# Second layer's heads: score and value products as three fp32r products, woven into the next head's value projection

## The chip, the cores and the metric

The kernel runs on one core of a Trainium2 chip. The metric is the device time of one execution in microseconds (us); of several executions the median counts.

## The reference, cut to what matters

The program runs four layers and then a second block over 256 latent and 256 context tokens of width 2048, all in f32. The change is in layer 1, a bidirectional mLSTM with 8 heads. Scores are 128 wide per head, values 256:

```python
def _mlstm_branch(h_lat, h_ctx, w_in, b_gate, hn, w_out, ctx_out):
    q, k, v, o, g, z = jnp.split(h @ w_in, idx, axis=-1)
    ...
    s = jnp.einsum('bhtd,bhsd->bhts', q, k) * jnp.exp(dmat - m_t[..., None])
    num = a[..., None] * jnp.einsum('bhtd,bhde->bhte', q, C) + jnp.einsum('bhts,bhse->bhte', s, v)
    den = a * jnp.einsum('bhtd,bhd->bht', q, n) + jnp.sum(s, axis=-1)
    h = num / jnp.maximum(jnp.abs(den), jnp.exp(-m_t))[..., None]
    ...
    y = jax.nn.sigmoid(o) * h
    y = _rmsnorm(y, hn)
    return (y * jax.nn.silu(z)) @ w_out
```

The scan over chunks is computed here as one masked product over all 512 tokens in each of the two directions (d = 0 forward, d = 1 backward): P = exp(cb + column) x (k q), masked, then P times [v, 1], whose last column is the denominator.

## The kernel before

Each engine has its own program, written out by hand; they meet in semaphores. `L.up(..., name)` marks an event, `w.wait_ge(L.at(name))` waits for it. An engine works strictly in the order in which its program is written.

**Projections.** Weights come in pieces of 1024 columns (half a 128x2048 block). A piece is loaded into WR, ScalarE rounds it to fp32r in WH (L1574), VectorE writes the rest WR - WH to WL (L2389); TensorE then makes three fp32r products of it with the activations HH and HL (`three`, L502 to L506, and `tproject`, L635 to L637). WH and WL hold three pieces (`NP` = 3), so a piece can be split only when TensorE is through with the third before it. `cut_to(n)` on ScalarE and VectorE splits all pieces below n; `along(job)` is `cut_to` of the job's last piece plus 3. One piece is 24 products of 512 columns.

**One head h on TensorE**, in order: two products that spread `cb` over a bank each (PS4, PS5; L1038), the score product S(h,0), z projection 2h, S(h,1), z projection 2h+1, S(h,2), q(h+1), S(h,3), k(h+1), then the value products (L1061: 20 of them, two directions for each of four token blocks tb, in banks PS4 to PS7 in turn), then `vo(h+1)` (values and output gate of the next head, 8 pieces, four banks at once), then eight transposes of the result M_HH (L1072). z, z, q, k take one accumulating bank each of PS0 to PS3, and `vo` takes all four: its fourth bank is that of k. `tproject` asks for all its banks, and waits for them, before its first product. Head 7 has no q, k and vo behind it.

**VectorE in a head**: `cb` plus a column into M_P (L2363), M_P times S out of PSUM (L2360, `mult` below), the splits, the drain of the value products (three small instructions for the denominator and one of 256 columns, L2366 or L2369, for each tb and direction), M_HH times the gate (L2360, 1024 columns), the norm (L2366), then the evacuation of the transposes (L2369) and of the values (L2372). Between them it works at `bg(n)`: n steps of the vector-matrix products for the modulations of later layers (L2411; two passes of 1024 columns a step while both the latent and the context vector need it, one pass in the last part). Each step's block of `ada_w` is loaded by SyncE into one of two buffers when the step before the last is through. ScalarE does the exps, tanhs, squares and the evacuation of q, k and the gate; GpSimd masks the diagonal blocks.

The four score blocks are called k = 0 to 3 (key block), with columns 0 to 512 for k < 2, 256 to 512 else.

## Time and profile before

| what | value |
|---|---|
| median of 3 runs | 2987.71 us (2981.6 to 2988.95) |
| the profiled execution's own time | 2990.57 us |
| its span, first to last instruction | 2988.8 us |
| TensorE busy | 2932.5 us (98%) |
| VectorE busy | 2090.1 us (70%) |
| ScalarE busy | 1178.0 us (39%) |
| granted TensorE clock | 0.996 of full speed |

Busy times are those of one execution; the value "idle before" counts gaps above 0.15 us. A matmul's duration is its latency; neighbours overlap, so what one costs is the distance of two starts.

### The profile page before, as it was taken

What the parts mean: (1) busy time and instruction counts of PE and PEld (TensorE: products, weight loads), DVE (VectorE), ACT (ScalarE), POOL (GpSimd) and SP (SyncE); (2) the same over time, 40 slices, a digit from 0 to 9 for tenths busy, and PEclk for the clock granted to TensorE, in tenths of its full rate; (3) what the DMA queues carried; (4) which work ended last, traced back from release to release, by engine and by line L of the source; (5) the groups of instructions that cost most, each with busy time, mean ns of one, the idle gap of its engine ahead of it and who ended that gap; (6) DMA issues with size and microseconds to landing.
All of it is one profiled execution on the core that took longest, in us unless ns stands there. A gap on an engine that the chain in (4) does not pass through costs nothing.

```text
span 2988.8 us, 43582 instructions
## 1 busy us (share of the span) xinstructions
PE 2932.5 (98%) x17098; PEld 2353.5 (79%) x17098; DVE 2090.1 (70%) x3957; ACT 1178.0 (39%) x2056; POOL 103.5 (3%) x188
## 2 busy tenths in 40 slices
PE   8999999999999999999999999999999999999999
PEld 7777778888888888878888888888888888885346
DVE  4576876788888776677666886677675678765455
ACT  4322323322332232242245555455444445543344
POOL 0000000000000000000000000000010120000000
PEclk9999999999999999999999999999999999999999
DMA  9777784354555455538636774645576443487997
GB/s 366 281 266 286 273 282 149 127 169 148 190 168 177 162 183 169 179 128 275 235 117 206 258 241 142 197 148 180 195 236 218 141 164 128 152 274 259 403 404 314
DMA packets 193197, 641.69 MB, mean 215 GB/s; under 512 B 21488, under 2 KB 36192, under 8 KB 192992
## 3 DMA queue, kind: packets, MB, share of 16 engines
q1 hardware_dynamic: 132080, 423.44, 40.6%
q10 hardware_dynamic: 58032, 207.12, 20.3%
q0 software_dynamic: 2880, 8.35, 0.9%
q8 instruction: 135, 2.21, 0.3%
q14 instruction: 70, 0.57, 0.1%
HBM read 624.15 MB, written 12.58 MB: 213 GB/s over the span
## 4 chain that ended last, share of the span: by engine, by line
PE 87%; DVE 7%; ACT 3%; DMA 2%; issue 1%; SPq 0%; DVEq 0%; ACTq 0%; POOL 0%; POOLq 0%
PE PS L506 15%; PE PS L502 11%; PE PS L504 9%; PE PS L505 9%; PE PS L635 7%; PE PS L637 7%; PE PS L636 7%; PE PS L1061 2%; PE PS L798 2%; PE PS L1472 2%; DMA AR<-e_w 1%; DVE WL L2389 1%; PE PS L1441 1%; PE PS L1428 1%; PE PS L1122 1%
## 5 line engine op out<-in xcount | busy, mean ns | idle before, releaser
L2389 DVE TENSOR_TENSOR WL<-WR,WH 128x1024 fp32r<-128x1024 f32 (+1 forms) x566 | 682.4, 1211 | 401.7 <-ACT WH L1574 400.5
L506 PE MATMUL PS<-HT,WL 128*128 128x256 f32 (+1 forms) x2928 | 951.5, 325 | 0.0
L1574 ACT ACTIVATE WH<-WR 128x1024 fp32r<-128x1024 f32 (+1 forms) x566 | 587.1, 1044 | 873.1 <-PE PS L506 486.7
L506 PEld LDWEIGHTS PS<-HT,WL 128*128 128x128 f32 x2928 | 552.1, 189 | 47.6
L502 PE MATMUL PS<-HT,WH 128*128 128x512 f32 x1584 | 566.0, 401 | 9.2 <-DVE WL L2389 6.1
L504 PE MATMUL PS<-HT,WH 128*128 128x512 f32 (+1 forms) x1344 | 518.4, 386 | 5.4 <-DVE HT L2369 2.4
L505 PE MATMUL PS<-HT,WH 128*128 128x512 f32 (+1 forms) x1344 | 507.9, 378 | 0.0
L635 PE MATMUL PS<-WH,HT 128*128 128x512 f32 x1016 | 402.7, 396 | 3.5 <-DVE HT L2369 2.5
L637 PE MATMUL PS<-WH,HT 128*128 128x512 f32 x1016 | 396.8, 391 | 0.0
L636 PE MATMUL PS<-WL,HT 128*128 128x512 f32 x1016 | 396.2, 390 | 0.0
L502 PEld LDWEIGHTS PS<-HT,WH 128*128 128x128 f32 x1584 | 297.4, 188 | 90.2 <-issue 13.1
L504 PEld LDWEIGHTS PS<-HT,WH 128*128 128x128 f32 x1344 | 253.1, 188 | 70.1 <-issue 14.6
L505 PEld LDWEIGHTS PS<-HT,WH 128*128 128x128 f32 x1344 | 253.3, 188 | 47.2 <-issue 1.7
L635 PEld LDWEIGHTS PS<-WH,HT 128*128 128x128 f32 x1016 | 191.3, 188 | 42.8 <-DVE HT L2369 2.1
L637 PEld LDWEIGHTS PS<-WH,HT 128*128 128x128 f32 x1016 | 191.1, 188 | 40.5
L636 PEld LDWEIGHTS PS<-WL,HT 128*128 128x128 f32 x1016 | 191.2, 188 | 38.2
L2411 DVE CUSTOM_DVE_ANT_0 WR<-WR,SCB,MOD 128x1024 f32<-128x1024 f32 x132 | 169.3, 1283 | 20.3 <-DMA WR<-ada_w 16.5
L2411 DVE CUSTOM_DVE_ANT_0 WR<-WR,SCB 128x1024 f32<-128x1024 f32 x132 | 161.4, 1223 | 23.5 <-DMA WR<-ada_w 19.9
L2369 DVE SCALAR_TENSOR_TENSOR YT<-PS,MOD,YT 128x256 f32<-128x256 f32 x126 | 57.9, 481 | 56.0 <-PE PS L506 54.5
L2411 DVE CUSTOM_DVE_ANT_0 JUNK<-WR,SCB,MOD 128x1024 bf16<-128x1024 f32 x68 | 87.0, 1280 | 4.0 <-DMA WR<-ada_w 1.9
L2411 DVE CUSTOM_DVE_ANT_0 JUNK<-WR,SCB 128x1024 bf16<-128x1024 f32 x68 | 83.0, 1220 | 5.9 <-DMA WR<-ada_w 3.4
L2360 DVE TENSOR_TENSOR AR<-AR 128x512 f32<-128x512 f32 (+9 forms) x140 | 74.3, 535 | 10.0 <-ACT AR L1705 1.2
(472 smaller groups left out, 3319.1 us busy)
## 6 DMA issues: line engine op xcount, KB each, us to landing
WR<-ada_w SPq DMA_DIRECT2D x264, 512.0 KB, 4.6
AR<-e_w SPq DMA_DIRECT2D x88, 512.0 KB, 10.0
E_RING<-e_w SPq DMA_DIRECT2D x80, 512.0 KB, 10.2
WR<-m_vo ACTq DMA_DIRECT2D x64, 512.0 KB, 4.6
WR<-a_qz ACTq DMA_DIRECT2D x64, 512.0 KB, 4.8
WR<-n_m SPq DMA_DIRECT2D x64, 512.0 KB, 4.3
AR<-ada_p ACTq DMA_DIRECT2D x56, 512.0 KB, 6.3
AR<-ada_p SPq DMA_DIRECT2D x48, 512.0 KB, 8.0
```

The source lines that it names most:

```text
L502: e.matmul(ps[:, 0:512], wh, HT[:, :, c, a:b], start=c == 0, stop=False)
L504: e.matmul(ps[:, 0:b - a], wh, HH_[:, c, a:b], start=c == 0, stop=False)
L505: e.matmul(ps[:, 0:b - a], wh, HL_[:, c, a:b], start=False, stop=False)
L506: return e.matmul(ps[:, 0:b - a], wl, HH_[:, c, a:b], start=False, stop=c == last)
L635: e.matmul(ps[:], HH_[:, c, t], wh[:, k, :], start=c == 0, stop=False)
L636: e.matmul(ps[:], HH_[:, c, t], wl[:, k, :], start=False, stop=False)
L637: i = e.matmul(ps[:], HL_[:, c, t], wh[:, k, :], start=False, stop=c == 15)
L798: i = e.matmul(ps[32 * k:32 * k + 32, 256 * half:256 * half + 256], S2Q[:, at:at + 32], wa[:, k, :], start=m == 0, stop=m == GP - 1)
L1574: e.activation(part_of(WH, s), place_of(plan["slot"][p])[:, 0:width(s)], ACT.Copy, scale=1.0).then_inc(*L.up(hi_done, ("hi", s)))
L2360: e.tensor_tensor(o, a, b, op).then_inc(*done(*names))
L2389: e.tensor_tensor(part_of(WL, s), place_of(plan["slot"][plan["split"][s]])[:, 0:width(s)], part_of(WH, s).bitcast(F32), ALU.subtract).then ...
L2411: e.tensor_tensor_reduce(out=o, in0=x, in1=SCB[:, v, k], scale=1.0, scalar=m if half else 0.0, op0=ALU.mult, op1=ALU.add, accum_out=m).the ...
```

## The change

The score product S(h,k) and each value product, plain f32 matmuls before, become three fp32r products of high and low parts (high x high, high x low, low x high). For that ScalarE writes high parts (M_QH, M_VH, M_PH) and VectorE low parts (M_QL, M_VL, M_PL: `q_low`, `k_low`, `lows`). The value products get 258 columns instead of 257. The four token blocks of value products are issued behind pieces 0 to 3 of `vo(h+1)`, no longer ahead of it. The addition of the column to `cb` goes from VectorE to ScalarE (Identity, or at once as bias of the exp), the masks are applied before the exp, the first direction's scaling (`first_way`) and the norm (`normed`) go to ScalarE; P is held only in the blocks that the mask leaves (M_BLOCKS, 2560 of 3072 columns). q and k have one buffer instead of two.

```diff
-    M_QK = [cv(1024, "p (a n) -> p a n", a=2) for _ in range(2)]
-    M_V = cv(4 * 257, "p (t n) -> p t n", t=4)
+    M_QH, M_QL = (ARR[:, 1024 * i:1024 * i + 1024].rearrange("p (a n) -> p a n", a=2) for i in range(2))
+    cv(2048)
+    cv(4 * 258)
     M_O = cv(1024, "p (t n) -> p t n", t=4)
     M_HH = cv(1024, "p (t n) -> p t n", t=4)
     M_P = [cv(1536) for _ in range(2)]
     M_E2 = cv(512)
+    M_VH, M_VL = (ARR[:, at:at + 1032].rearrange("p (t n) -> p t n", t=4) for at in (2048, 11784))
+    M_PH = [ARR[:, 8712 + 1536 * d:10248 + 1536 * d] for d in range(2)]
+    M_PL = [ARR[:, 5128 + 1536 * d:6664 + 1536 * d] for d in range(2)]
...
-            def vo(h):
-                tproject(("vo", h), I["m_vo"][h], 1, ALL, acc if h else wrk)
+            def vo(h, between=()):
+                tproject(("vo", h), I["m_vo"][h], 1, ALL, acc if h else wrk, between)
...
-                    w.wait_ge(L.at(("qe", h), ("ke", h)))
-                    e.matmul(ps[:, 0:512 - c0], qk[:, 1, 128 * k:128 * k + 128], qk[:, 0, c0:512], start=True,
-                             stop=True).then_inc(*L.up(mm_done, ("full", ("S", h, k)), ("qk_used", h)))
+                    w.wait_ge(L.at(("ql", h), ("kl", h)))
+                    o, t = ps[:, 0:512 - c0], slice(128 * k, 128 * k + 128)
+                    e.matmul(o, M_QH[:, 1, t], M_QH[:, 0, c0:512], start=True, stop=False)
+                    e.matmul(o, M_QH[:, 1, t], M_QL[:, 0, c0:512], start=False, stop=False)
+                    e.matmul(o, M_QL[:, 1, t], M_QH[:, 0, c0:512], start=False, stop=True).then_inc(
+                        *L.up(mm_done, ("full", ("S", h, k)), ("qk_used", h)))
...
-                for tb in range(4):
+                def value_products(tb):
                     for d in range(2):
                         ps = bank(4 + (2 * tb + d) % 4, ("pv", h, tb, d))
                         ks = M_KEYS[tb][d]
                         for m, k in enumerate(ks):
                             c = M_PC[k] + 128 * tb - (0 if k < 2 else 256)
-                            w.wait_ge(L.at(("p", h, k, d), ("ve", h), ("one", "v")))
-                            i = e.matmul(ps[:, 0:257], M_P[d][:, c:c + 128], M_V[:, k, :], start=m == 0,
-                                         stop=m == len(ks) - 1)
+                            ph, pl = M_PH[d][:, c:c + 128], M_PL[d][:, c:c + 128]
+                            w.wait_ge(L.at(("p", h, k, d), ("ve", h)))
+                            e.matmul(ps[:, 0:258], ph, M_VH[:, k, :], start=m == 0, stop=False)
+                            e.matmul(ps[:, 0:258], ph, M_VL[:, k, :], start=False, stop=False)
+                            i = e.matmul(ps[:, 0:258], pl, M_VH[:, k, :], start=False, stop=m == len(ks) - 1)
                         i.then_inc(*L.up(mm_done, ("full", ("pv", h, tb, d)), ("p_used", h), ("v_used", h)))
+
                 if h < 7:
-                    vo(h + 1)
+                    vo(h + 1, {tb: lambda tb=tb: value_products(tb) for tb in range(4)})
                 else:
+                    for tb in range(4):
+                        value_products(tb)
...
+                e.activation(M_QH[:, 0, :], place[("q", h)][:], ACT.Copy, scale=ASC).then_inc(*L.up(act_done, ("qe", h)))
...
+                e.activation(M_QH[:, 1, :], place[("k", h)][:], ACT.Copy, scale=1.0).then_inc(*L.up(act_done, ("ke", h)))
...
+                    e.activation(M_VH[:, tb, 0:256], place[("vo", h, tb)][:, 0:256], ACT.Copy, scale=1.0).then_inc(
+                        *L.up(act_done, ("vh", h, tb)))
                     e.activation(M_O[:, tb, :], place[("vo", h, tb)][:, 256:512], ACT.Tanh, scale=0.5).then_inc(
                         *L.up(act_done, ("oe", h), ("oe", h, tb), ("free", ("vo", h, tb))))
...
+                for d in range(2):
+                    ps, free = place[("cb", h, d)], ("free", ("cb", h, d))
+                    w.wait_ge(L.at(("full", ("cb", h, d))))
+                    for k in range(4):
+                        t = slice(128 * k, 128 * k + 128)
+                        e.activation(M_P[d][:, m_at(k, t.start, t.stop)], ps[:, t], ACT.Identity,
+                                     bias=M_ACOL[:, k, 32 * d + h:32 * d + h + 1], scale=1.0).then_inc(
+                            *L.up(act_done, ("pt", h, k, d), free))
+                    for k in range(4):
+                        for a, b in M_REST[k, d]:
+                            e.activation(M_P[d][:, m_at(k, a, b)], ps[:, a:b], ACT.Exp,
+                                         bias=M_ACOL[:, k, 32 * d + h:32 * d + h + 1], scale=1.0).then_inc(
+                                *L.up(act_done, ("pe", h, k, d), free))
                 for k in range(4):
-                    n = 512 if k < 2 else 256
                     for d in range(2):
-                        p = M_P[d][:, M_PC[k]:M_PC[k] + n]
-                        w.wait_ge(L.at(("pt", h, k, d)))
...
+                    for d in range(2):
+                        w.wait_ge(L.at(("pp", h, k, d)))
+                        for a, b in M_BLOCKS[k, d]:
+                            at = m_at(k, a, b)
+                            e.activation(M_PH[d][:, at], M_P[d][:, at], ACT.Copy, scale=1.0).then_inc(
+                                *L.up(act_done, ("ph", h, k, d)))
...
+                def first_way(tb):
+                    if h and tb == 0:
+                        w.wait_ge(L.at(("hh_used", h - 1)))
+                    w.wait_ge(L.at(("pvs", h, tb, 0)))
+                    e.activation(M_HH[:, tb, :], place[("pv", h, tb, 0)][:, 0:256], ACT.Copy,
+                                 scale=M_ST[2 * tb % 4][:, 0:1]).then_inc(
+                        *L.up(act_done, ("pvx", h, tb), ("free", ("pv", h, tb, 0))))
...
+                def normed():
+                    w.wait_ge(L.at(("yi", h)))
+                    for tb in range(4):
+                        e.activation(M_HH[:, tb, :], M_HH[:, tb, :], ACT.Copy, scale=s[:, 8 + tb:9 + tb]).then_inc(
+                            *L.up(act_done, ("yn", h, tb)))
...
+                    for q in range(8):
+                        cut_to(plan[("vo", h + 1)][0] + q + NP)
+                        if q < 4:
+                            first_way(q)
+                        elif q == 4:
+                            squares()
+                        elif q == 5:
+                            normed()
...
-                    copy(M_V[:, tb, 0:256], place[("vo", h, tb)][:, 0:256], ("ve", h), ("free", ("vo", h, tb)))
+                    w.wait_ge(L.at(("vh", h, tb), ("oe", h, tb)))
+                    tt(M_VL[:, tb, 0:256], place[("vo", h, tb)][:, 0:256], M_VH[:, tb, 0:256].bitcast(F32), ALU.subtract,
+                       ("ve", h), ("free", ("vo", h, tb)))
...
+            def q_low(h):
+                w.wait_ge(L.at(("qe", h)))
+                stt(M_QL[:, 0, :], place[("q", h)][:], ASC, M_QH[:, 0, :].bitcast(F32), ALU.mult, ALU.subtract, ("ql", h),
+                    ("free", ("q", h)))
+
+            def k_low(h):
+                w.wait_ge(L.at(("ke", h)))
+                tt(M_QL[:, 1, :], place[("k", h)][:], M_QH[:, 1, :].bitcast(F32), ALU.subtract, ("kl", h),
+                   ("free", ("k", h)))
...
+                def lows(k):
+                    for d in range(2):
+                        w.wait_ge(L.at(("ph", h, k, d)))
+                        for a, b in M_BLOCKS[k, d]:
+                            at = m_at(k, a, b)
+                            tt(M_PL[d][:, at], M_P[d][:, at], M_PH[d][:, at].bitcast(F32), ALU.subtract, ("p", h, k, d))
...
-                        p = M_P[d][:, M_PC[k]:M_PC[k] + 512 - c0]
-                        ts(p, place[("cb", h, d)][:, c0:512], M_ACOL[:, k, 32 * d + h:32 * d + h + 1], 0.0,
-                           ALU.add, ALU.min, ("pt", h, k, d), *([("free", ("cb", h, d))] if k == 3 else []))
...
+                        q_low(h + 1)
+                lows(3)
+                if h < 7:
+                    k_low(h + 1)
...
+                def drained(tb):
                     for d in range(2):
...
+                        recip(s, s, ("pvs", h, tb, d))
+                        if d:
+                            w.wait_ge(L.last(dve_done), L.at(("pvx", h, tb)))
                             stt(M_HH[:, tb, :], ps[:, 0:256], s, M_HH[:, tb, :], ALU.mult, ALU.add,
                                 ("free", ("pv", h, tb, d)))
...
+                    for q in range(8):
+                        cut_to(plan[("vo", h + 1)][0] + q + NP)
+                        if q < 4:
+                            drained(q)
+                        if q == 3:
+                            opened()
+                            bg(1)
+                        elif q == 5:
+                            inverse()
+                        bg(1)
...
-                        w.wait_ge(L.at(("pe", h, k, d)))
-                        e.affine_select(out=pd, in_=pd, compare_op=ALU.is_ge, fill=0.0, base=0,
+                        w.wait_ge(L.at(("pt", h, k, d)))
+                        e.affine_select(out=pd, in_=pd, compare_op=ALU.is_ge, fill=-3e38, base=0,
...
```

VectorE's program between k(h+1) and the drain, head 1. WL is a split, ISA a pass of `bg`, PS1 the bank of k(2), PS0 that of q(2). Before:

```order
L2389 TENSOR_TENSOR WL<-WR,WH 128x1024 [waits hi_done] x2
L2411 ISA JUNK,MOD<-WR,SCB,MOD 128x1024 [waits ada_done,adaw1_landed]
L2411 ISA MOD 128x1
L2411 ISA WR,MOD<-WR,SCB,MOD 128x1024 [waits ada_done]
L2411 ISA MOD 128x1
L2411 ISA JUNK,MOD<-WR,SCB 128x1024 [waits ada_done,adaw0_landed]
L2411 ISA MOD 128x1
L2411 ISA WR,MOD<-WR,SCB 128x1024 [waits ada_done]
L2411 ISA MOD 128x1
L2369 SCALAR_TENSOR_TENSOR SML<-PS4,SML 128x1 [waits mm_done]
```

and in the changed program:

```order
L2462 TENSOR_TENSOR WL<-WR,WH 128x1024 [waits hi_done] x2
L2484 ISA JUNK,MOD<-WR,SCB,MOD 128x1024 [waits ada_done,adaw1_landed]
L2484 ISA MOD 128x1
L2484 ISA WR,MOD<-WR,SCB,MOD 128x1024 [waits ada_done]
L2484 ISA MOD 128x1
L2484 ISA JUNK,MOD<-WR,SCB 128x1024 [waits ada_done,adaw0_landed]
L2484 ISA MOD 128x1
L2484 ISA WR,MOD<-WR,SCB 128x1024 [waits ada_done]
L2484 ISA MOD 128x1
L2442 SCALAR_TENSOR_TENSOR ARR<-PS0,ARR 128x512 [waits act_done]
L2433 TENSOR_TENSOR ARR<-AR,ARR 128x128 [waits act_done]
L2433 TENSOR_TENSOR ARR<-AR,ARR 128x256 [waits act_done]
```

Behind the last row stand the low part of k, which releases PS1, then a split, then the first drain. q's and k's low parts and the last low parts of P have moved in behind the two `bg` steps.

TensorE, from the last products of k(2) on. Before, the value products (L1061) followed, and vo (L635) behind them:

```order
L506 MATMUL PS1<-HT,WL 128x512
L1061 MATMUL PS4<-AR 128x257
L1061 MATMUL PS5<-AR 128x257 x2
L1061 MATMUL PS6<-AR 128x257 [waits dve_done]
L1061 MATMUL PS6<-AR 128x257
```

and in the changed program vo (L648) follows at once, with a wait for VectorE:

```order
L519 MATMUL PS1<-HT,WL 128x512
L648 MATMUL PS2<-WH,HT 128x512 [waits dve_done,lo_done]
L649 MATMUL PS2<-WL,HT 128x512
L650 MATMUL PS2<-WH,HT 128x512
L648 MATMUL PS2<-WH,HT 128x512
```

The value products now come 24 products later, and nothing stands between k and the wait for its bank.

ScalarE, the evacuation of vo, before:

```order
L1888 ACT_TABLE_LOAD
L1888 ACTIVATE AR<-PS2 128x256 [waits mm_done]
L1888 ACTIVATE AR<-PS3 128x256
L1888 ACTIVATE AR<-PS0 128x256
L1888 ACTIVATE AR<-PS1 128x256
```

and in the changed program, where the load of tanh's table has moved from ahead of the wait for vo to behind the first copy:

```order
L1909 ACTIVATE ARR<-PS2 128x256 [waits mm_done]
L1911 ACT_TABLE_LOAD
L1911 ACTIVATE AR<-PS2 128x256
L1909 ACTIVATE ARR<-PS3 128x256
L1911 ACTIVATE AR<-PS3 128x256
```

## Rows read from the trace of the kernel before

**Rows 1.** The page: busy time of two engines, and the chain that ended last

```profile
PE 2932.5 (98%) x17098; PEld 2353.5 (79%) x17098; DVE 2090.1 (70%) x3957; ACT 1178.0 (39%) x2056; POOL 103.5 (3%) x188
...
PE 87%; DVE 7%; ACT 3%; DMA 2%; issue 1%; SPq 0%; DVEq 0%; ACTq 0%; POOL 0%; POOLq 0%
```

**Rows 2.** Windows, two heads, two value stretches, a head's start, head 7

```profile
core 0: us, PE busy (x) PEld busy (x) DVE busy (x) ACT busy (x) POOL busy (x), PEclk, DMA share, GB/s
684.25:785.32 101.07, 100.49 (x444) 82.12 (x443) 82.72 (x148) 28.47 (x43) 3.41 (x9) 1.00 0.52 172
1188.81:1289.07 100.26, 100.26 (x444) 82.21 (x443) 61.68 (x113) 28.46 (x43) 3.41 (x9) 1.00 0.53 173
833.30:842.65 9.35, 8.77 (x42) 7.33 (x40) 8.31 (x32) 0.60 (x1) 0.00 (x0) 1.00 0.35 112
1236.80:1245.30 8.50, 8.50 (x42) 7.41 (x40) 6.21 (x28) 0.60 (x1) 0.00 (x0) 1.00 0.30 101
785.32:787.79 2.47, 2.47 (x13) 1.39 (x12) 1.84 (x4) 1.21 (x4) 0.98 (x1) 1.00 0.61 182
1302.55:1314.35 11.80, 10.49 (x48) 8.47 (x46) 9.84 (x37) 0.60 (x1) 0.00 (x0) 1.00 0.26 89
```

**Rows 3.** Timeline of TensorE, end of k(3), value products, start of vo(3)

```profile
start us, us, engine line op out<-in xcount [idle before <-releaser]
832.85 0.39 PE L505 MATMUL PS<-HT,WH 128*128 128x512 f32 x1
833.07 0.39 PE L506 MATMUL PS<-HT,WL 128*128 128x512 f32 x1
833.30 2.77 PE L1061 MATMUL PS<-AR 128*128 128x257 f32 x12
836.64 6.35 PE L1061 MATMUL PS<-AR 128*128 128x257 f32 x28 [0.58 <-DVE SML L2369]
842.65 0.58 PE L635 MATMUL PS<-WH,HT 128*128 128x512 f32 x1
```

**Rows 4.** Timeline of TensorE, fp32r products of 256 columns in another layer

```profile
1496.96 0.28 PE L710 MATMUL PS<-HT,WH 128*128 128x256 f32 x1
1497.08 0.28 PE L711 MATMUL PS<-HT,WH 128*128 128x256 f32 x1
1497.20 0.28 PE L712 MATMUL PS<-HT,WL 128*128 128x256 f32 x1
```

**Rows 5.** Timeline of ScalarE, evacuation of k(3)

```profile
833.50 0.60 ACT L1879 ACTIVATE AR<-PS 128x512 f32<-128x512 f32 x1 [4.32 <-PE PS L506]
```

**Rows 6.** Timeline of VectorE around k(3)'s end, a heavy head

```profile
829.21 1.23 DVE L2389 TENSOR_TENSOR WL<-WR,WH 128x1024 fp32r<-128x1024 f32 x1 [3.16 <-ACT WH L1574]
830.35 1.22 DVE L2411 CUSTOM_DVE_ANT_0 JUNK<-WR,SCB 128x1024 bf16<-128x1024 f32 x1
...
834.32 1.28 DVE L2411 CUSTOM_DVE_ANT_0 WR<-WR,SCB,MOD 128x1024 f32<-128x1024 f32 x1
835.52 0.08 DVE L2411 DVE_READ_ACCUMULATOR2_ANT MOD<- 128x1 f32 x1
835.52 0.15 DVE L2369 SCALAR_TENSOR_TENSOR SML<-PS,SML 128x1 f32<-128x1 f32 x1
...
836.50 0.15 DVE L2369 SCALAR_TENSOR_TENSOR SML<-PS,SML 128x1 f32<-128x1 f32 x1
```

**Rows 7.** Timeline of VectorE, instructions like the new ones

```profile
801.77 0.68 DVE L2369 SCALAR_TENSOR_TENSOR YT<-AR,PS 128x512 f32<-128x512 f32 x1
802.37 1.28 DVE L2360 TENSOR_TENSOR AR<-AR,PS 128x512 f32<-128x512 f32 x2
...
824.17 0.74 DVE L2360 TENSOR_TENSOR AR<-AR,PS 128x256 f32<-128x256 f32 x2
824.83 1.22 DVE L2389 TENSOR_TENSOR WL<-WR,WH 128x1024 fp32r<-128x1024 f32 x1
```

**Rows 8.** Timeline of VectorE around k(6)'s end (1136.55), a light head

```profile
1136.18 0.08 DVE L2411 DVE_READ_ACCUMULATOR2_ANT MOD<- 128x1 f32 x1
1137.18 0.16 DVE L2369 SCALAR_TENSOR_TENSOR SML<-PS,SML 128x1 f32<-128x1 f32 x1 [0.92 <-PE PS L1061]
```

**Rows 9.** The loads of ada_w from 600 to 1300 us

```profile
DMA to landing us min/median/max: 3.5/4.3/7.3
```

**Rows 10.** Timeline of VectorE behind the end of vo(2) at 785.32

```profile
785.95 1.41 DVE L2369 SCALAR_TENSOR_TENSOR YT<-PS,SML,YT 128x512 f32<-128x512 f32 x2 [0.97 <-PE PS L1072]
```

**Rows 11.** Timeline of ScalarE ahead of vo(1)'s evacuation

```profile
679.06 1.06 ACT L1574 ACTIVATE WH<-WR 128x1024 fp32r<-128x1024 f32 x1 [4.38 <-PE PS L637]
680.14 1.28 ACT L1888 ACT_TABLE_LOAD   x1
684.45 1.21 ACT L1888 ACTIVATE AR<-PS 128x256 f32<-128x256 f32 x4 [3.03 <-PE PS L637]
```

More of the change, by code:

```diff
@@ L1934, in mlstm @@
                     vo(h + 1)
                 else:
+                    for tb in range(4):
+                        first_way(tb)
+                    squares()
+                    normed()
                     z_(15)
@@ L2906, in along_vo @@
                     bg(1)
+            def q_low(h):
[6 more added lines that the diff above has]
+                   ("free", ("k", h)))
+            q_low(0)
+            k_low(0)
             z_(0)
@@ L2969, in mlstm, with opened, inverse @@
-                if h < 7:
-                    along_vo(h + 1, 0)
-                else:
+                def opened():
+                    w.wait_ge(L.last(dve_done), L.at(("oe2", h)))
+                    tt(M_HH[:], M_HH[:], M_O[:], ALU.mult, ("yo", h), ("o_used", h))
+                def inverse():
+                    w.wait_ge(L.at(("yr", h)))
+                    recip(st[:, 8:12], st[:, 8:12], ("yi", h))
+                if h < 7:
+                    for q in range(8):
[8 more added lines that the diff above has]
+                        bg(1)
+                else:
+                    for tb in range(4):
+                        drained(tb)
+                    opened()
+                    inverse()
```

96 lines of the change are left out of this document (44 added, 52 removed).

## The prediction

> **What bounds the kernel now.** I read the page first: TensorE is busy for 98% of the span and carries 87% of the chain that ended last, VectorE for 70% [rows 1]. Then windows over one head: the head from 684.25 to 785.32 us lasts 101.07 us with TensorE busy for 100.49 and VectorE for 82.72; the head from 1188.81 lasts 100.26 with VectorE at 61.68 [rows 2]. The difference is background work: in five heads a `bg` step is two passes of 1024 columns (0 to 4; "heavy"), in heads 5 and 6 one pass ("light"). TensorE is thus the limit, so two things count: how many columns it issues less, and whether something makes it stand. Where it stands now can be seen in the value products: 9.35 us in a heavy head, with one idle of 0.58 behind VectorE's drain, 8.50 in a light one for the same 40 instructions [rows 2, 3].
>
> **What the products save.** A plain f32 product is two instructions, so 8.50/40 = 0.2125 us each and 0.425 for 257 columns [rows 2]. fp32r products of 256 columns start every 0.12 us, those of 512 every 0.23 [rows 3, 4]. Twenty value products a head become 60 x 0.12 = 7.2 us. The first fp32r instruction behind f32 takes 0.58 instead of 0.39 [rows 3], 0.19 that goes too. So the value products save 9.35 - 7.2 + 0.19 = 2.35 in a heavy head, 1.5 in a light one. Scores: 512 columns 2 x 0.43 = 0.86 become 3 x 0.227 = 0.68, 256 columns 0.43 become 0.36; S1 to S3 give 0.3 and with their switches 0.5. Together 2.85 us (heavy) and 2.0 (light). No row shows 258 columns; the bounds are the 256 row and, in proportion, half of the 512 row (0.114 to 0.121), under 0.5 us a head either way.
>
> The Trainium skill (FP8 and Floating Point Precision, TensorE Precision Notes) says that true FP32 is four passes through the array, so three would take 3/4. By it the 8.50 would become 6.4, 0.8 us a head better than by the rows; the rows (0.12 against 0.2125 for twice the passes) show a fixed part in each instruction, and they decide.
>
> **What the move costs first: k's bank.** `vo(h+1)` takes all four accumulating banks before its first product, and the fourth holds k(h+1). Before, the value products stood between k and vo and hid k's way out: ScalarE's copy began 0.2 us behind k's end at 833.30 and took 0.60 [rows 5]. Now vo stands directly behind k, and the bank is released only by `k_low` on VectorE, which is queued behind bg(2), `q_low` and `lows(3)`. Where VectorE is then, the trace shows: it waits 3.16 us for the half-matrix that TensorE frees in the middle of k, splits it (829.21), and its bg(2) runs from 830.35 to 835.52, that is until 2.22 us behind k's end [rows 6]. That is tied to TensorE's own k, so a relieved VectorE doesn't bring it forward, it only waits longer than 3.16. Behind it: `q_low` 0.60 (row 801.77 to 802.37), `lows(3)` 128 and 256 columns, at most 0.2 + 0.33 (824.17, two in 0.66), `k_low` 0.68, and 0.1 for the semaphore: 2.22 + 0.60 + 0.53 + 0.68 + 0.1 = 4.1 us of standing TensorE in each of five heads [rows 6, 7]. In light heads the bg ends 0.3 before k's end (1136.26 against 1136.55; behind it VectorE waits for the first value product) [rows 8], and the way is 0.2 + 0.6 + 0.7 + 0.1 = 1.6 us, twice. Total 23.7 us, against 5 x 2.85 + 2 x 2.0 = 18.3 saved.
>
> **Second: the end of vo.** Count from vo's start, heavy head. VectorE splits one piece (1.14), then waits for the first value product: 24 x 0.227 + 3 x 0.12 + 0.3 = about 6.0. From there per step: a drain 1.1 to 1.7 (before 0.98 for each of two), a bg 2.6, a split 1.14 [rows 6]. With its waits for the products at 13, 20 and 28 this gives the third product set drained at 22.4, the fourth at 30.3, `opened` at 31.5, two bg at 36.7, split 37.8 (TensorE needs it at 6 x 5.45 + 7.2 = 39.9), then 40.4, 41.5, 44.4, 45.5, 48.1, 49.2, 51.8. vo ends at 43.6 + 7.2 = 50.8 and the first transposed bank is full at 51.4. One more delay is likely: the two bg in a row release a load buffer at 34.1, the next load lands 4.3 us later (3.5 to 7.3) at 38.5, and the bg at 37.8 waits 0.7 for it [rows 9]; that makes 52.5. Before, VectorE waited 0.97 for those transposes, and z's first product started 2.47 behind vo's end [rows 2, 10]. Now the two evacuations (0.67 each) and the first low value part (0.4) follow 1.65 after vo's end: z starts at 3.5. In light heads ScalarE sets it: the table load for tanh, 1.28 us, was done 3 us ahead of need [rows 11] and now stands between the first value copy and the first tanh, at 0.2 + 0.4 + 1.28 + 0.4 + 0.4 = 2.8. So +1.0 (heavy), +0.3 (light).
>
> The Trainium skill (ScalarE: Activation LUTs, What ACT_TABLE_LOAD costs) adds a drain of about 1380 ns to each 1283 ns load. By it z would start at 4.1 instead; here the row shows 1.28, and the load starting 0.02 behind the copy ahead of it (679.06 + 1.06 to 680.14), so the sum leaves the drain out and a rival below takes it in.
>
> **What stays hidden.** ScalarE gets about 9 us of work a head, but it is busy for 28 of 101 [rows 2]. Its longest new stretch at a head's start (eight copies and tanhs, eight identities, seven exps, eight more behind GpSimd's masks, then the first copies of P) ends some 9.2 us behind vo's end and the split of z1's first piece at 11.5; TensorE wants it at 3.5 + 10.9 + 0.7 = 15. If that 3.5 us of cover were gone, each us over it would cost seven. VectorE loses 4.2 us of sums from `cb` and gains about as much in low parts; in the z, q and k stretches this fits in its waits, of which the last is the 3.16.
>
> **Ends.** Head 7 has no vo to weave into. Between z's end and the end of its value products now lie 11.80 us [rows 2]. The chain mult, ScalarE copy, low part for k = 1, 2, 3 runs until about 7.4, before anything is drained, and banks 4 and 5 come free only then; I get 13.5, so +1.7, with its evacuation +1.9. Head 0: eight ScalarE pieces instead of four ahead of the `cb` products, +0.7.
>
> **Sum.** Heavy: -2.85 + 4.1 + 1.0 = +2.25, x5 = 11.2. Light: -2.0 + 1.6 + 0.3 = -0.1, x2. Ends +2.6. Total +13.6, say +13. The profiled execution took 2990.57 us, 2.9 above the median of the three runs shown; 2990.6 + 13 = 3004 on its scale, 3001 on that of the median, which is my number.
>
> **Rivals.**
> A, no wait at k's bank and VectorE on time at vo's end: 5 x (0.3 - 2.85) + 2 x (0.3 - 2.0) + 2.6 = -13.5, 2974 us. It takes a VectorE that is through with bg(2) before k ends; light heads speak for it, the five heavy ones against (2.22 behind). The point from which it decides is a wait under 1.9 us in heavy heads. Chance 0.07.
> B, gain and waits nearly cancel: the products save 0.6 more a head (towards the lower bound), no load is late and z starts at 2.8: 5 x (4.1 + 0.3 - 3.45) + 2.6 - 1.4 = +6 or less, 2991 to 2994. Chance 0.22.
> C, VectorE's backlog breaks through: the split that TensorE needs at 39.9 has 2.1 us of cover, less 0.7. If loads take 5.3 or the drains 0.5 more each, that cover is gone, TensorE stands inside vo and again at its end, 2 to 3 us more in each heavy head: +24 to +28, 3012 to 3015. Chance 0.14.
> D, the switch of ScalarE's table costs another 1.38 us between first copy and first tanh (a drain ahead of the load): z starts at 4.1 in every head, 5 x 0.6 + 2 x 1.3 = +5.6, 3006 us. The 0.02 us in front of the load speaks against it. The same skill page as above is its source. Chance 0.05.
> The forecast itself has 0.52, between 2995 and 3007.
>
> **Numbers.** 0.3% is 9 us, about what a measurement of this kernel can tell from no change; slower begins at 2997. Slower: 0.43 of the forecast's 0.52, C and D: 0.62. Same: the rest of the forecast and B: 0.31. Faster: A, 0.07. The range leaves out A and the far half of C: 2986 to 3013.
>
> **What would show it.** Right: idle on TensorE before the first L648 product of each vo, ended by VectorE's tensor-tensor, about 4 us five times and 1.5 twice; value products (L1077 to L1079) starting every 0.12; ACT_TABLE_LOAD of 1.28 directly behind the first L1909 of a head; the step from vo's end to z at 3 to 3.5 us; heads of about 103.3 and 100.2 us. Wrong: heads under 100 us in the first five, or idle before L517 or L650 groups inside z, q, k or vo with a split (WL) as releaser, which would mean that my cover for the splits isn't there.

## The result, and the profile after

| | before | after |
|---|---|---|
| median | 2988.33 us (2981.6 to 2989.35, 4 runs) | 3028.69 us (3027.75 to 3031.97, 4 runs) |
| span of the profiled execution | 2988.8 us | 3026.4 us |
| heads 1 to 4, end of `vo` to end of `vo` | 404.31 us | 432.72 us |

The ratio is 1.014 (95% interval 1.0128 to 1.0152): slower by 40 us, on the side that was predicted, with three times the size. The page of the changed kernel, against [rows 1]: TensorE is busy for 5.5 us less and still carries less of the chain, because VectorE's share of it has grown.

```profile
PE 2927.0 (97%) x17290; PEld 2357.7 (78%) x17290; DVE 2067.6 (68%) x3926; ACT 1254.9 (41%) x2344; POOL 101.7 (3%) x188
...
PE 76%; DVE 13%; ACT 6%; DMA 2%; issue 2%; SPq 1%; DVEq 0%; ACTq 0%; POOL 0%; POOLq 0%
```

Windows give the place: a heavy head and a light one from one end of `vo` to the next, as in [rows 2] (length first, then busy time and count of PE, PEld, DVE, ACT and POOL, then the granted clock, DMA share and GB/s).

```profile
688.69:797.34 108.65, 101.28 (x468) 83.97 (x467) 79.50 (x143) 38.14 (x79) 3.09 (x9) 0.95 0.49 160
1121.41:1222.10 100.69, 98.58 (x468) 82.03 (x467) 58.92 (x108) 37.99 (x79) 3.10 (x9) 1.00 0.54 176
```

A light head is 0.4 us longer than before and this heavy one 7.6; heads 1 to 4 last 108.65, 107.13, 108.11 and 108.83, 7.1 more on average. In the heavy one TensorE is idle for 7.4 us and, with less work, busy for longer at a mean clock of 0.95. Both come at one place, the start of `vo`. Here it is in the next heavy head on TensorE; a row gives start, duration and instruction, and in brackets the idle time before it and what ended it:

```profile
852.00 0.77 PE L648 MATMUL PS<-WH,HT 128*128 128x512 f32 x1 [6.06 <-DVE ARR L2433]
852.57 0.63 PE L649 MATMUL PS<-WL,HT 128*128 128x512 f32 x1
...
853.42 0.63 PE L648 MATMUL PS<-WH,HT 128*128 128x512 f32 x1
...
856.12 0.39 PE L650 MATMUL PS<-WH,HT 128*128 128x512 f32 x1
856.35 0.40 PE L648 MATMUL PS<-WH,HT 128*128 128x512 f32 x1
...
859.10 0.28 PE L1077 MATMUL PS<-ARR 128*128 128x258 f32 x1
...
859.34 0.28 PE L1079 MATMUL PS<-ARR 128*128 128x258 f32 x1
```

Two things are to be seen: 6.06 us of standing that ends with VectorE's tensor-tensor (`k_low`), and after it products that start every 0.43 us instead of every 0.23, for more than 3 us. Windows over the stand and the first piece of the head before show the clock:

```profile
736.66:743.75 7.09, 0.16 (x2) 0.04 (x1) 6.88 (x13) 1.65 (x2) 0.00 (x0) 0.68 0.75 247
743.75:751.97 8.22, 8.22 (x25) 6.51 (x25) 0.87 (x1) 0.00 (x0) 0.00 (x0) 0.65 0.14 46
```

The granted clock falls to half (1.2 of 2.4 GHz) during the stand and comes back 3 to 6 us into the piece, which takes 8.22 us where a piece at full clock takes about 5.5. While TensorE stands, VectorE is busy for 6.88 of 7.09 us. What it does in the third head's stand (k ends at 845.8):

```profile
839.86 0.62 DVE L2433 TENSOR_TENSOR ARR<-AR,ARR 128x256 fp32r<-128x256 f32 x2
840.40 0.61 DVE L2433 TENSOR_TENSOR AR<-AR,PS 128x128 f32<-128x128 f32 x2
842.44 2.36 DVE L2462 TENSOR_TENSOR WL<-WR,WH 128x1024 fp32r<-128x1024 f32 x2 [1.43 <-ACT WH L1594]
844.72 1.22 DVE L2484 CUSTOM_DVE_ANT_0 JUNK<-WR,SCB 128x1024 bf16<-128x1024 f32 x1
...
848.69 1.28 DVE L2484 CUSTOM_DVE_ANT_0 WR<-WR,SCB,MOD 128x1024 f32<-128x1024 f32 x1
849.90 0.69 DVE L2442 SCALAR_TENSOR_TENSOR ARR<-PS,ARR 128x512 fp32r<-128x512 f32 x1
850.50 0.61 DVE L2433 TENSOR_TENSOR ARR<-AR,ARR 128x128 fp32r<-128x128 f32 x2
851.03 0.68 DVE L2433 TENSOR_TENSOR ARR<-PS,ARR 128x512 fp32r<-128x512 f32 x1
```

The split waits 1.43 us for ScalarE's WH and then covers two half-matrices at once; bg(2) makes way for `q_low` at 849.90, 4.1 us behind k, and `lows(3)` and `k_low` follow. In the five heavy heads this lateness is 4.4, 5.0, 4.1, 3.7 and 4.9 us, mean 4.4; before it was 2.2 in each. ScalarE in the same stretch shows why WH was late:

```profile
840.71 0.75 ACT L1957 ACTIVATE ARR<-AR 128x128 fp32r<-128x128 f32 x2 [4.97 <-DVE AR L2433]
841.37 1.99 ACT L1594 ACTIVATE WH<-WR 128x1024 fp32r<-128x1024 f32 x2
845.99 0.60 ACT L1900 ACTIVATE ARR<-PS 128x512 fp32r<-128x512 f32 x1 [2.62 <-PE PS L519]
```

It stood for 4.97 us at its copy of P, which needs VectorE's `mult` of 840.40; the two rounded half-matrices are queued behind that copy. The buffer of the first had been free since TensorE began with k (834.88), that of the second since the middle of k, some 5.5 us later. VectorE's next split then waits for them. Two in-order engines thus wait for each other in turn, and VectorE enters k's end late.

**Accounts.** From `vo` to `vo`, a heavy head costs 6.5 us of waiting (6.5, 7.1, 6.2, 5.8 and 7.0, from k's end to the first product of `vo`; the row's idle is up to 0.2 less), 2.4 of slow clock (first piece 7.72, 8.22, 7.10, 8.11 and 8.45 against 5.49), 0.8 at z's start (2.90, 3.39, 3.79 and 2.91 in heads 1 to 4, mean 3.25, against 2.47), and saves the predicted 2.85: +6.9, where the trace has (432.72 - 404.31)/4 = 7.1. Head 0 went from 90.90 to 97.81, heads 5 and 6 together from 200.51 to 201.34, head 7 from 38.07 to 42.71. That is 6.9 + 28.4 + 0.8 + 4.6 = 40.7; the part of the program ahead of head 0 was 2.5 us shorter in this execution and the part behind head 7 by 0.7, in code that the change doesn't touch.

### The profile page after: what moved, and what is told of

It reads as the page before. It is cut to its first block, busy times and chain, and to the rows that moved or that the text cites. A ratio compares the mean times of both kernels' runs of the same rounds, so it can differ in the third digit from the quotient of the medians.

```text
span 3026.4 us, 44332 instructions
## 1 busy us (share of the span) xinstructions
PE 2927.0 (97%) x17290; PEld 2357.7 (78%) x17290; DVE 2067.6 (68%) x3926; ACT 1254.9 (41%) x2344; POOL 101.7 (3%) x188
## 4 chain that ended last, share of the span: by engine, by line
PE 76%; DVE 13%; ACT 6%; DMA 2%; issue 2%; SPq 1%; DVEq 0%; ACTq 0%; POOL 0%; POOLq 0%
PE PS L519 12%; PE PS L515 11%; PE PS L648 7%; PE PS L650 7%; PE PS L649 7%; PE PS L517 7%; PE PS L518 7%; DVE WL L2462 3%; DVE WR L2484 2%; DMA AR<-e_w 2%; PE PS L811 2%; DVE JUNK L2484 2%; ACT WH L1594 1%; PE PS L1492 1%; PE PS L1461 1%
## 5 line engine op out<-in xcount | busy, mean ns | idle before, releaser
L648 PE MATMUL PS<-WH,HT 128*128 128x512 f32 x1016 | 407.7, 401 | 38.6 <-DVE ARR L2433 35.1
L650 PE MATMUL PS<-WH,HT 128*128 128x512 f32 x1016 | 401.1, 395 | 0.0
L648 PEld LDWEIGHTS PS<-WH,HT 128*128 128x128 f32 x1016 | 194.2, 191 | 80.8 <-DVE ARR L2433 37.8
L1973 ACT ACTIVATE AR<-PS,SML 128x256 f32<-128x256 f32 x32 | 15.2, 474 | 211.9 <-DVE SML L2448 211.9
```

Source lines behind the costliest of these rows:

```text
L648: e.matmul(ps[:], HH_[:, c, t], wh[:, k, :], start=c == 0, stop=False)
L650: i = e.matmul(ps[:], HL_[:, c, t], wh[:, k, :], start=False, stop=c == 15)
```

## The experiments

What I took to be true before these runs: the whole loss in heavy heads is k's bank, held by VectorE behind bg(2), plus the clock that the stand costs; VectorE's lateness is 2.2 us from its own queue and the rest from the ring of waits with ScalarE. The rivals: the weaving itself is what costs, or the clock alone is.

**1. VectorE's background step behind `k_low`.** Does the work queued ahead of the release make the loss?

```diff
                         along(("k", h + 1))
-                        bg(2)
                         q_low(h + 1)
                 lows(3)
                 if h < 7:
                     k_low(h + 1)
+                    bg(2)
```

> The changed kernel with one edit: in the k stretch VectorE's two bg steps come behind q_low, lows(3) and k_low instead of ahead of them. Theory 1 (the bank of k is released late because 5.2 us of bg stand ahead of k_low): the wait ahead of vo falls in the five heavy heads from 6.5 us (mean) to about 1.8, as in the light ones, and with it goes the loss in vo's first piece (2.4 us a head at the lower clock): 5 x (6.5 + 2.4 - 1.8) = 35 us less, 2993 us. Theory 2 (VectorE has too much work in a heavy head, wherever it stands): the 5.2 us come back behind k_low, as late splits or a later z, and less than half is gained: over 3010 us.

Measured: 2993.1 us (2989.4 to 2996.34, 10 runs), ratio 1.0018 (1.0008 to 1.0027). One statement on VectorE takes back 35.6 of the 40.4 us. The heavy heads last 100.69 to 101.36 us, the light ones 100.63, and TensorE waits 1.61 in place of 6.06. First the heavy head's window, then TensorE's first product of `vo`:

```profile
784.47:885.16 100.69, 98.58 (x468) 82.05 (x467) 78.87 (x143) 38.15 (x79) 3.11 (x9) 1.00 0.51 171
```

```profile
834.24 0.47 PE L648 MATMUL PS<-WH,HT 128*128 128x512 f32 x1 [1.61 <-DVE ARR L2433]
```

The first piece takes 5.53 to 5.57 us and the clock reads 1.00: a stand of 1.6 us leaves it alone. A heavy head has the same busy time and count on TensorE as a light one and is only 0.3 us longer on average, so the background's second pass costs hardly anything once it isn't ahead of the release. The 1.6 is the bare chain of semaphore, ScalarE's copy and `k_low`.

**2. ScalarE's splits ahead of its copies of P.** Does the ring with ScalarE make the difference between the 4.1 that I had predicted and the 6.5?

```diff
                 for k in range(4):
+                    nxt = ("z", 2 * h) if k == 0 and h else {1: ("z", 2 * h + 1), 2: ("q", h + 1), 3: ("k", h + 1)}.get(k) if h < 7 else None
+                    if nxt:
+                        cut_to(ahead(nxt) - 1)
                     for d in range(2):
```

> The changed kernel with one edit: ScalarE makes the high part of the first weight piece of each z, q and k stretch ahead of its copies of P instead of behind them. In the changed kernel VectorE waits 1.4 to 1.7 us in each stretch for ScalarE, which copies P only when VectorE has multiplied it and splits only then. Theory 1 (this ring of waits is what makes VectorE 4.1 us late at k's end in place of the 2.2 of before): the wait ahead of vo falls from 6.5 to about 4.3 us and the clock's share with it, 3010 to 3015 us. Theory 2 (VectorE is late from its own new work, the low parts): the waits only move, the wait ahead of vo stays at 6 or more, 3025 us or more.

Measured: 3015.49 us (3012.49 to 3019.24, 4 runs), ratio 1.0089 (1.0073 to 1.0106). With the 0.23 of a product's own distance taken off, TensorE waits 4.3, 4.6, 4.3, 4.3 and 4.3. The mean is 4.36. VectorE in the k stretch of one head now splits the two half-matrices apart, and the second waits for the one that TensorE frees in the middle of k, as before in [rows 6]:

```profile
834.22 1.22 DVE L2465 TENSOR_TENSOR WL<-WR,WH 128x1024 fp32r<-128x1024 f32 x1
...
836.93 1.23 DVE L2465 TENSOR_TENSOR WL<-WR,WH 128x1024 fp32r<-128x1024 f32 x1 [1.50 <-ACT WH L1594]
```

That is the picture on which the 4.1 rested: VectorE's lateness at k's end is 2.2 us in four of the heavy heads and 2.5 in one, as before, and the 4.1 holds within 0.3. But the first piece still takes 7.1 to 8.0 us: 4.3 us of standing cost the clock nearly as much as 6.5.

**3. TensorE kept busy while it waits.** 27 products of the identity into a free bank (6 in the light heads) ahead of `vo`; nothing else changes.

```diff
                 if h < 7:
+                    w.wait_ge(L.at(("free", ("cb", h, 0))))
+                    keep_warm(psum[4], 27 if h < 5 else 6)
                     vo(h + 1, {tb: lambda tb=tb: value_products(tb) for tb in range(4)})
```

> The changed kernel with filler on TensorE ahead of each vo: 27 products of 128 columns with the identity in heads 0 to 4, 6 in heads 5 and 6, into a bank that is free (about 6 us, within the wait for k's bank; they compute nothing that is used). Theory 1 (standing for 6.5 us lets the granted clock fall to 0.5, and vo's first piece pays for it): the first piece takes 5.5 us instead of 7.1 to 8.5, the end of the wait stays where it was, 12 us less, 3017 us. Theory 2 (the first piece is slow for another reason, late pieces or banks): no change, 3029 us.

Measured: 3012.3 us (3011.35 to 3014.68, 4 runs), ratio 1.0083 (1.0066 to 1.0099), 16 less than the changed kernel. This measures the clock's cost apart from the wait. TensorE's filler and the first product behind it, then windows over filler and first piece:

```profile
733.10 6.19 PE L658 MATMUL PS<-IDN 128*128 128x128 f32 x54
...
740.23 0.47 PE L648 MATMUL PS<-WH,HT 128*128 128x512 f32 x1 [0.94 <-DVE ARR L2435]
```

```profile
734.00:740.20 6.20, 5.29 (x48) 5.10 (x47) 5.99 (x13) 1.06 (x1) 0.00 (x0) 1.00 0.78 260
740.20:745.80 5.60, 5.57 (x25) 4.64 (x26) 0.88 (x1) 0.00 (x0) 0.00 (x0) 1.00 0.16 59
```

`vo` starts 7.13 us behind k's end as in the changed kernel (7.09), since VectorE's queue is the same, but its first piece takes 5.54 instead of 8.22. The five first pieces give 11.9 us. Of the 16.9 between the two profiled executions the rest lies outside the heavy heads: 1.4 us ahead of head 0 and 3.8 behind the last `vo`, in code that the edit doesn't touch. So 12 of the 16 are shown to be the clock's, and the other 4 are not.

**4. The weaving undone, all else kept.** The value products stand in one block ahead of `vo` again, and the drains on ScalarE and VectorE move with them.

```diff
+                for tb in range(4):
+                    value_products(tb)
                 if h < 7:
-                    vo(h + 1, {tb: lambda tb=tb: value_products(tb) for tb in range(4)})
+                    vo(h + 1)
...
```

> The changed kernel with the value products back ahead of vo, in one block as before, and the drains on ScalarE and VectorE in one block behind the first split. All products stay fp32r. Theory 1 (what costs is VectorE's lateness at k's end, not the weaving): the first two product sets (2.2 us) run, the third waits for a drained bank until about 7.9 us behind k's end, vo starts at about 12.6: 5.4 us lost in place of 6.5, 3020 to 3028 us. Theory 2 (weaving is the cost, since it takes the cover from k's bank): the block hides the bank as before and heads take 99 to 100 us, 2975 to 2985 us.

Measured: 3022.7 us (3020.79 to 3026.15, 4 runs), ratio 1.0115 (1.0099 to 1.0132). The wait doesn't go, it moves into the block of value products, ahead of the third token block. Its first product takes the bank of the first set, which VectorE and ScalarE must have drained. TensorE's rows, then VectorE's and ScalarE's ahead of them:

```profile
853.12 0.58 PE L1077 MATMUL PS<-ARR 128*128 128x258 f32 x1 [6.24 <-ACT AR L1973]
853.50 0.42 PE L1078 MATMUL PS<-ARR 128*128 128x258 f32 x1
```

```profile
849.15 0.69 DVE L2443 SCALAR_TENSOR_TENSOR ARR<-PS,ARR 128x512 fp32r<-128x512 f32 x1
...
850.89 1.22 DVE L2463 TENSOR_TENSOR WL<-WR,WH 128x1024 fp32r<-128x1024 f32 x1
...
852.40 0.17 DVE L2449 RECIPROCAL SML<-SML 128x1 f32<-128x1 f32 x1
```

```profile
852.60 0.47 ACT L1973 ACTIVATE AR<-PS,SML 128x256 f32<-128x256 f32 x1 [6.27 <-DVE SML L2449]
```

VectorE comes to `q_low` at 849.15, 4.6 us behind k's end (844.57). The low parts, one split and the drain's small instructions follow, and ScalarE's drain is the last link. The low parts of `lows(3)` are done before 850.4, and the product at 853.12 doesn't need them. Here too products start at half speed behind the stand (0.22 for 258 columns instead of 0.12). So the weaving isn't what costs the 40 us: VectorE comes late out of its background work, and whatever TensorE needs of it first, k's bank or a drained one, is late with it.

**5. The weaving alone, in the kernel before.** Products in plain f32, high and low parts and the work on ScalarE left out; only the order of value products, drains and `vo`'s pieces is that of the changed kernel.

```diff
                 if h < 7:
-                    vo(h + 1)
+                    vo(h + 1, {tb: lambda tb=tb: value_products(tb) for tb in range(4)})
...
```

> The kernel before with the weaving alone: plain f32 products, P, q and k as before, but the value products behind vo's pieces 0 to 3 and VectorE's drains in the same places. Theory 1 (weaving is harmless while ScalarE alone releases k's bank, and costs only what VectorE is late at vo's end): the wait ahead of vo is about 0.8 us, PE's waits inside the value products (0.6 to 0.9 us a heavy head) go, z starts 1.5 to 2.5 us later in heavy heads; 2995 to 3003 us. Theory 2 (weaving by itself makes the long wait ahead of vo): 3015 us or more.

Measured: 2996.86 us (2995.01 to 2999.95, 7 runs), ratio 1.0027 (1.0016 to 1.0038). The weaving costs 8 to 9 us by itself. Part of it is k's bank with its bare release, without VectorE in the way:

```profile
733.09 0.47 PE L635 MATMUL PS<-WH,HT 128*128 128x512 f32 x1 [0.89 <-ACT AR L1881]
```

Counted from k's end it is 1.05 us in six heads and 1.13 in one, 7.4 us in all. Heavy heads last 102.4 to 103.1, light ones 101.5 to 101.7.

**6. Two of the four token blocks ahead of `vo`.** With experiment 1's order on VectorE, token blocks 0 and 1 (18 of the 60 value products) go ahead of `vo` and 2 and 3 behind its pieces 1 and 2; the drains follow.

```diff
+                    for tb in range(2):
+                        value_products(tb)
-                    vo(h + 1, {tb: lambda tb=tb: value_products(tb) for tb in range(4)})
+                    vo(h + 1, {1: lambda: value_products(2), 2: lambda: value_products(3)})
...
```

> The kernel with bg behind k_low, and the value products of token blocks 0 and 1 moved back ahead of vo (18 products, 2.15 us); blocks 2 and 3 come behind vo's pieces 1 and 2, with the drains moved alike. Theory 1 (what is left of the wait, 1.8 us by 7, is the way of k's bank through ScalarE and VectorE, and any 2 us of other products cover it): the wait ahead of vo is gone, 12.5 us less than with bg behind alone (2993.1), 2980 us. Theory 2 (the two blocks wait themselves, for their low parts or for banks): the wait moves ahead of them, no more than 4 us gained.

Measured: 2981.03 us (2979.16 to 2984.11, 10 runs), ratio 0.9978 (0.9969 to 0.9988). Now it is faster than before the change. TensorE stands for 0.5 us in a head, at z's start:

```profile
781.13:879.89 98.76, 98.26 (x467) 82.12 (x466) 79.70 (x144) 38.16 (x79) 3.11 (x9) 1.00 0.53 179
```

The 2.15 us of these 18 products are enough to cover the 1.6 us of k's way out, and the drains, begun earlier, are all done before `vo` ends. The gain over experiment 1 is 12.1 us, or 1.7 in each of seven heads.

**7. The table of tanh loaded early.** Experiment 1's kernel, and one tanh of one column ahead of ScalarE's wait for `vo`. The column that it writes holds a gain of a later layer, so the kernels of experiments 7 to 9 overwrite that gain: the work and its order are right, the result is not. In the changed kernel the load stands between the first copy and the first tanh:

```profile
797.53 0.38 ACT L1909 ACTIVATE ARR<-PS 128x256 fp32r<-128x256 f32 x1 [4.32 <-PE PS L650]
797.94 1.28 ACT L1911 ACT_TABLE_LOAD   x1
799.23 0.38 ACT L1911 ACTIVATE AR<-PS 128x256 f32<-128x256 f32 x1
```

```diff
                 along(("vo", h))
+                if h:
+                    e.activation(SML[:, 639:640], EPSC[:], ACT.Tanh, scale=1.0).then_inc(*L.up(act_done))
                 w.wait_ge(L.at(("full", ("vo", h))))
```

> The kernel with bg behind k_low, and one tanh of a single column ahead of ScalarE's wait for vo, so that the table of tanh is loaded before vo ends. Theory 1 (the table load stands on the way of z's bank): z starts 2.3 to 2.5 us behind vo's end instead of 2.9, 3 to 4 us less than 2993.1, 2989.5 us. Theory 2 (the wait for the transposed bank's evacuation sets z's start anyway): no change that can be measured, 2992 to 2994 us.

Measured: 2988.73 us (2987.17 to 2992.43, 10 runs), ratio 1.0005 (0.9996 to 1.0014), 4.4 less than experiment 1. ScalarE's rows ahead of a light head's end of `vo` show the load out of the way:

```profile
1183.29 1.28 ACT L1905 ACT_TABLE_LOAD   x1
1184.58 0.20 ACT L1905 ACTIVATE SML<-EPSC 128x1 f32<-128x1 f32 x1
1187.59 0.38 ACT L1911 ACTIVATE ARR<-PS 128x256 fp32r<-128x256 f32 x1 [2.81 <-PE PS L650]
```

z starts 0.43 us earlier in the heads 5 and 6 and 0.78 in head 7, where it waits for ScalarE. In heads 1 to 4 it is 0.2 to 0.4 earlier three times and 0.3 later once. Together that is 2.2 us; where the other 2.2 come from these two executions don't show.

**8. All four edits together** (1, 2, 6 and 7).

> All four edits on the changed kernel: bg behind k_low, ScalarE's first split ahead of its copies of P, the tanh ahead of vo, value blocks 0 and 1 ahead of vo. Theory 1 (the waits are independent): the gains add up, 2993.1 - 12.5 - 3.5 = 2977 us, 0.4% faster than the kernel before. Theory 2 (VectorE's work in a head is near its limit, so a wait taken away shows up elsewhere): 2983 us or more.

Measured: 2973.83 us (2972.44 to 2975.74, 5 runs), ratio 0.9957 (0.9944 to 0.9971), 3 us better than the sum of the gains. Heads last 98.33 to 98.59.

**9. The same, and head 7's value products behind the first piece of z 15.**

```diff
...
-                    for tb in range(4):
-                        value_products(tb)
-                    z_(h, 1)
+                    z_(h, 1, [(0, lambda: [value_products(tb) for tb in range(4)])])
```

> As the kernel with all four edits, and in head 7 the value products come behind the first of the two pieces of z 15 instead of ahead of it (5.4 us of cover for the chain of VectorE and ScalarE that they wait for). Theory 1 (TensorE's wait of 4.6 + 0.8 us in head 7 is hidden by that piece, but the transposes now come 5.4 us sooner behind the drains, which need 8 to 9 us): 2 to 3 us less than with the four edits. Theory 2 (all of it comes back ahead of the transposes): no change against the four edits.

Measured: 2981.33 us (2974.38 to 2983.65, 8 runs), ratio 0.9977 (0.9966 to 0.9987): 7.5 more, where 2 to 3 less was expected. The wait ahead of S(7,3) stays (3.74 us from the end of the product ahead of it; it lies ahead of the moved block), and the drains come later, so that the transposes wait 1.4 and the output projection 3.3 for VectorE, where there had been 0.9 for the latter:

```profile
1311.91 1.87 PE L1092 MATMUL PS<-IDN,AR 128*128 128x128 f32 x8 [1.44 <-ACT AR L1996]
...
1317.08 0.77 PE L517 MATMUL PS<-HT,WH 128*128 128x512 f32 x1 [3.30 <-DVE HT L2443]
```

z 15 was the cover of the drains' end; with its first piece ahead of the block, less of it is left behind. These waits are 3.9 us more than before; in the 24 us behind 1311 the granted clock was also 0.86 where experiment 8 with another scratch column (experiment 10) has 1.00 from the same point on, and what of the 7.5 is the clock's can't be told apart here. The eight executions suggest that it is a good part: the five with a mean clock of 0.993 to 0.995 took 2981.16 to 2983.65 us, the three with 0.996 or 0.997 took 2974.38 to 2978.84.

**10. Experiment 8 with another column as the target of the tanh.** Nothing else uses this column, so the gain stays.

> The kernel with all four edits once more, with one column moved: the tanh ahead of vo wrote into a column that holds a gain of a later layer, so the outputs of the three kernels with it (the one with the tanh alone on top of bg behind, the one with four edits, the one with z 15) are not the reference's; it now writes into a column that nothing uses. Nothing in this changes an instruction's size or place. Both theories of the run with four edits expect the same time as there, 2972 to 2976 us; 0.4% faster than the kernel before.

Measured: 2974.93 us (2972.42 to 2976.99, 5 runs), ratio 0.9952 (0.9938 to 0.9965): 13 to 14 us faster than the kernel before, 54 faster than the changed one. Windows of a heavy and a light head:

```profile
780.39:878.73 98.34, 98.27 (x467) 82.13 (x466) 79.41 (x144) 38.35 (x80) 3.12 (x9) 1.00 0.54 178
1173.79:1272.13 98.34, 98.27 (x467) 82.14 (x466) 58.31 (x109) 38.46 (x80) 3.11 (x9) 1.00 0.55 177
```

TensorE is busy for 98.27 of 98.34 us in both. The seven heads now hold nothing but its own work, 1.9 and 2.7 us less than in [rows 2].

**11. Experiment 10 without the background steps of z 14.** Is the remaining stand in head 7, 3.72 us ahead of S(7,3), VectorE's bg?

```diff
-                    bg(2 if n else 0)
+                    bg(2 if 0 < n < 14 else 0)
```

> As the kernel with all four edits, without the two bg steps of z 14, in head 7 (2.6 us of VectorE; they are made later, in the out projection). Theory 1 (TensorE's wait of 3.7 us ahead of the last score product in head 7 is VectorE being late by those two steps): 2 to 2.6 us less than with four edits, 2971 us. Theory 2 (VectorE waits there for ScalarE's copies and masks, or gives the time back in the out projection): no change.

Measured: 2975.86 us (2973.23 to 2976.43, 5 runs), ratio 0.9954 (0.994 to 0.9967): no change. The wait falls only from 3.72 to 2.86, and head 7 as a whole doesn't get shorter (40.09 against 39.41 us from `vo`'s end to its own transposes). The windows from S(7,3) to the end of the value products, experiment 10 first, show where the 0.86 went:

```profile
1290.24:1300.63 10.39, 9.50 (x63) 9.22 (x64) 7.94 (x34) 3.68 (x9) 0.00 (x0) 0.84 0.05 18
1289.88:1301.80 11.92, 11.02 (x63) 10.31 (x64) 8.00 (x34) 3.67 (x9) 0.00 (x0) 0.71 0.01 1
```

The same 63 products took 1.53 us more, at a granted clock of 0.71 instead of 0.84. The background steps are thus not the main part of that wait. What makes up the rest was not tested; by the program it is the chain of `mult`, ScalarE's copy and low part.

## Why the prediction was right or wrong

**Right in sign and in the kind of wait.** `vo` waits for k's bank, VectorE's tensor-tensor ends the wait, five times long and twice short: that is in the rows as predicted, and experiment 1 shows it to be 35.6 of the 40.4 us (with the clock that goes with it).

**Right in size, with some luck.** Value products start every 0.119 us, the 60 of a head take 7.15 (predicted 7.2). The light heads' wait is 1.8 (1.6). z's start is 2.90 in a light head (2.8) and 3.25 on average in a heavy one (3.5). That average is of two kinds: in heads 1 and 4 it is 2.90 and 2.91, as in a light head, and it is 3.39 and 3.79 in heads 2 and 3. Just these two have a load of `ada_w` that lands late, by 0.77 and 0.70 us, where I had 0.7 in every heavy head. The first of them is the last step of its `vo` and not the one that I had named:

```profile
796.35 1.28 DVE L2484 CUSTOM_DVE_ANT_0 JUNK<-WR,SCB,MOD 128x1024 bf16<-128x1024 f32 x1 [0.77 <-DMA WR<-ada_w]
```

The products' saving by rows, not by pass counts, held too: three products of 258 columns at 0.119 are 0.357 against 0.425, a ratio of 0.84. An estimate from the four passes that the Trainium skill (FP8 and Floating Point Precision, TensorE Precision Notes) states for true FP32 is 0.75; this case's trace doesn't agree. No drain stands around the table load: it begins 0.03 us behind the copy's end and the tanh 0.01 behind the load's, as in [rows 11], so rival D is false. The drain of which the Trainium skill (ScalarE: Activation LUTs, What ACT_TABLE_LOAD costs) speaks doesn't appear in this case's trace. What the load costs is 0.43 us of z's start in a light head (experiment 7). Rival C's mechanism, a split late inside `vo`, is false as well: no wait stands there.

**The first step that failed** is the sentence that VectorE's bg(2) at k's end "is tied to TensorE's own k", with 2.22 us of lateness. It was 3.7 to 5.0, mean 4.4. I had read the lateness off the trace of before, where the last split waits for the half-matrix that TensorE frees, and took it for fixed. The change put copies of P, which wait for VectorE, ahead of ScalarE's splits, and VectorE waits for the splits; by the end of the k stretch VectorE has lost its reserve: the 3.16 us of waiting that I counted as cover are 1.43, and those are spent on ScalarE. "What stays hidden" had asked only whether the new work fits into the idle time, and it does (VectorE 79.5 busy of 108.65); it hadn't asked who waits for whom. Experiment 2 removes the ring, and the lateness is 2.2 again and the wait 4.4: the term was right for an order of work that the changed kernel doesn't have. The rest of the term, 2.1 us of `q_low`, `lows(3)`, `k_low` and semaphore against a forecast of 1.9, was right. Cost: 2.4 us in five heads, 12 us.

**The second** is a term that I didn't have: a TensorE that has stood is slow afterwards. By the rows it costs 2.4 us in each heavy head, 12 in all, and experiment 3 gives those 12 back. A wait was priced at its own length only.

**A term of the sum that was too small**: the end in head 7. Its value stretch went from 11.80 to 15.86 us, predicted 13.5. S(7,3) stands behind k = 1's `mult`, which is queued behind the low parts of k = 0, and both behind the background steps of z 14. TensorE's row, and VectorE's around it:

```profile
1342.45 0.39 PE L1057 MATMUL PS<-ARR 128*128 128x256 f32 x1 [4.28 <-DVE AR L2433]
```

```profile
1336.94 1.28 DVE L2484 CUSTOM_DVE_ANT_0 WR<-WR,SCB,MOD 128x1024 f32<-128x1024 f32 x1
...
1339.52 0.68 DVE L2442 SCALAR_TENSOR_TENSOR YT<-AR,PS 128x512 f32<-128x512 f32 x1
1340.12 1.22 DVE L2433 TENSOR_TENSOR ARR<-AR,ARR 128x512 fp32r<-128x512 f32 x3
1341.26 1.14 DVE L2433 TENSOR_TENSOR AR<-AR,PS 128x384 f32<-128x384 f32 x2
```

I had taken the chain of k = 1 to 3 as free from the first score on; experiment 11 shows that taking the background steps away alone doesn't mend it. The larger part of the miss is the clock once more. Over S(7,3) and the value products it was 0.84, where the value stretch before the change has 1.00 [rows 2]:

```profile
1342.45:1352.85 10.40, 9.54 (x63) 9.12 (x64) 7.92 (x34) 3.68 (x9) 0.00 (x0) 0.84 0.06 22
```

That is 0.16 of 10.40 us, about 1.7, and leaves 0.7 for the chain.

**Sum of the misses**: 12.1 (ring) + 12.1 (clock) + 2.4 (head 7, 1.7 of it clock) = 26.6, of the 27.1 us between 13.6 forecast and 40.7 in the accounts above; the terms of z's start, of the light heads and of head 0 nearly cancel.

## What to carry to other kernels

When a change lets a busy in-order engine release what a faster one released before, count everything that is queued ahead of the release, and take into account that the work which used to stand between producer and next user may have been the cover. "The new work fits into the idle time" isn't enough: follow who waits for whom once around, since two engines that each have ample idle time can still hand each other their waits, and try the order that breaks the ring (splits first, background last) before giving up a change. A gain of 1.9 to 2.7 us a head was there; the places of a few statements decided between +1.4% and -0.5%. And price a stand by what the clock costs behind it too, not by its length alone.
